# A long convolution with its tables loaded a stage earlier and its phases in another order, and seven projections whose first weights are loaded in the stage before

## What is computed

```python
def hyena_filters(L, fw1, fb1, fw2, fb2, fw3, freq):
    ...
    h = jnp.sin(fq * (z @ fw1.astype(F32) + fb1.astype(F32)))
    h = jnp.sin(fq * (h @ fw2.astype(F32) + fb2.astype(F32)))
    h = h @ fw3.astype(F32)
    ...
    return h * (decay + HY_SHIFT)

def hyena_mix(u, conv_w, conv_b, filt, bias):
    u = dwconv(u, conv_w) + conv_b
    x0, x1, v = jnp.split(u, 3, axis=-1)
    g = (v * x1).astype(F32)
    h = hyena_filters(L, *filt)
    hf, hb = h[:, :HY_WIDTH], h[:, HY_WIDTH:]
    k2 = jnp.concatenate([hf, jnp.zeros((1, HY_WIDTH), F32), hb[:0:-1]], axis=0)
    n = 2 * L
    y = jnp.fft.irfft(jnp.fft.rfft(g, n=n, axis=1) * jnp.fft.rfft(k2, axis=0)[None], n=n, axis=1)[:, :L]
    y = y + g * bias.astype(F32)
    return y.astype(u.dtype) * x0
...
def conv_ffn(h, w_up, conv_w, conv_b, w_down):
    g, u = jnp.split(h @ w_up, 2, axis=-1)
    g = dwconv(g, conv_w) + conv_b
    return (jax.nn.silu(g) * u) @ w_down
```

## Time and profile before

| what | value |
|---|---|
| median of three runs | 3491.16 us (3490.48 to 3492.16) |
| the profiled execution, its own time | 3485.01 us |
| its span | 3483.2 us |
| TensorE busy | 3002.3 us, 86% |
| VectorE, ScalarE, GpSimd busy | 49%, 35%, 5% |
| TensorE's mean granted clock | 0.927 of full speed |
| moved by DMA | 362.79 MB, mean 104 GB/s |

### The profile page before, as it was taken

One profiled execution on the slowest core, in us unless ns is written; L12 is line 12 of the kernel. 1 busy time (PEld: TensorE's weight loads), 2 busy tenths in 40 slices (PEclk: granted clock), 3 DMA queues, 4 the chain that ended last, 5 costly groups with the idle time before them and its releaser, 6 DMA issues. The chain is left out here.

```text
span 3483.2 us, 38114 instructions
## 1 busy us (share of the span) xinstructions
PE 3002.3 (86%) x14263; PEld 2349.5 (67%) x14263; DVE 1699.8 (49%) x2349; ACT 1214.2 (35%) x1614; POOL 164.8 (5%) x131
## 2 busy tenths in 40 slices
PE   6896788978999999978999999978857788499996
PEld 2382367767888887756777887857635566477775
DVE  1343332354576643424564443341366554488886
ACT  0220022233323232423333442233323322377774
POOL 0000000110001100000000000000000100221210
PEclk9997899899999999989999999989978898699998
DMA  6311011011235333101002221212200013399996
GB/s 244 113 48 64 19 49 49 1 37 73 92 122 169 113 123 100 67 19 45 7 2 96 97 96 68 89 43 85 72 7 1 1 49 146 140 350 350 343 339 241
DMA packets 76311, 362.79 MB, mean 104 GB/s; under 512 B 13428, under 2 KB 17347, under 8 KB 50596
## 3 DMA queue, kind: packets, MB, share of 16 engines
q1 hardware_dynamic: 62404, 327.69, 26.6%
q0 software_dynamic: 13792, 33.58, 2.8%
HBM read 360.68 MB, written 16.27 MB: 108 GB/s over the span
## 5 line engine op out<-in xcount | busy, mean ns | idle before, releaser
L288 PE MATMUL ps<-rounded,rounded 128*128 128x512 f32 (+3 forms) x3700 | 1374.0, 371 | 108.7 <-DVE rounded L1978 24.1
L289 PE MATMUL ps<-rounded,rounded 128*128 128x512 f32 (+3 forms) x3700 | 1334.6, 361 | 0.0
L290 PE MATMUL ps<-rounded,rounded 128*128 128x512 f32 (+3 forms) x3700 | 1332.9, 360 | 0.0
L288 PEld LDWEIGHTS ps<-rounded,rounded 128*128 128x128 f32 (+1 forms) x3700 | 703.8, 190 | 284.8 <-issue 69.5
L290 PEld LDWEIGHTS ps<-rounded,rounded 128*128 128x128 f32 (+1 forms) x3700 | 704.1, 190 | 107.3
L289 PEld LDWEIGHTS ps<-rounded,rounded 128*128 128x128 f32 (+1 forms) x3700 | 705.7, 191 | 95.0
L267 DVE TENSOR_TENSOR rounded<-work,rounded 128x1024 fp32r<-128x1024 f32 (+3 forms) x224 | 306.4, 1370 | 817.5 <-ACT rounded L263 817.0
L263 ACT CAST rounded<-work 128x1024 fp32r<-128x1024 f32 (+3 forms) x224 | 260.8, 1166 | 701.2 <-PE ps L290 561.9
L3125 DVE TENSOR_TENSOR rounded<-work,rounded 128x2048 fp32r<-128x2048 f32 x138 | 311.7, 2288 | 91.1 <-ACT rounded L2973 88.5
L2973 ACT CAST rounded<-work 128x2048 fp32r<-128x2048 f32 x138 | 258.6, 1909 | 83.6 <-PE ps L290 83.6
L274 PE MATMUL ps<-cst 128*128 128x256 f32 x544 | 157.8, 455 | 105.2 <-PEq L169 105.2
(11 more groups left out here) (435 smaller groups left out, 2587.3 us busy)
## 6 DMA issues: line engine op xcount, KB each, us to landing
work<-in_moe SPq DMA_DIRECT2D x138, 1024.0 KB, 7.3
work<-in_ffn_up SPq DMA_DIRECT2D x44, 1024.0 KB, 4.8
work<-in_ffn_down SPq DMA_DIRECT2D x66, 512.0 KB, 3.5
work<-in_ada_w SPq DMA_DIRECT2D x12, 2048.0 KB, 8.6
work<-in_ada_w POOLq DMA_DIRECT2D x48, 512.0 KB, 4.1
work<-in_w_out SPq DMA_DIRECT2D x16, 512.0 KB, 3.5
work<-in_w_gates SPq DMA_DIRECT2D x16, 512.0 KB, 3.6
work<-in_w_in_hy SPq DMA_DIRECT2D x12, 512.0 KB, 3.3
```

The lines of the kernel that those rows point to most:

```text
L288: k.nc.tensor.matmul(out, sh, mh, start=start, stop=False)
L289: k.nc.tensor.matmul(out, sh, ml, start=False, stop=False)
L290: return k.nc.tensor.matmul(out, sl, mh, start=False, stop=stop)
```

## The change

**The tables of the convolution** (`HyenaRooms`) are loaded by the projection before it, behind its first two weight tiles (`also` of `project_conv`): the latent tables, both decays, both positions and the three weight matrices. Only the four small tables of the context are still loaded inside `hyena`, when the latent filters are done.

**The order of the convolution** is written out as one list, `groups`. Both lengths go through the filter network's first two layers together (768 columns). The sequences are transposed and transformed between these layers; each spectrum is copied out of PSUM by ScalarE; then follow the filters, and the filters' spectra are multiplied by it as they come. The context's phases lie between the latent ones. Every group waits only for what it reads.

**Seven projections** get their first two weight tiles in the stage before: the output gate of the first block (`w_in_og`), `w_z_2`, `w_gates_2` and `w_xbc_2` of the last one, and the down projections (context and latent of layer 0, latent of layer 1). Their streams use semaphores of their own that are never cleared, so their counts start from `base`. The stage before issues the loads (`then.begin`) and splits both tiles in its last turn (`then.high`, `then.low`), ScalarE ahead of taking the product out of PSUM. The seven stages have no warm-up matmuls any more.

```diff
@@ class Stream
+    def begin(self, sp, before=None):
         for s in range(self.n):
+            if before:
+                sp.wait_ge(before.ready[s], before.base + before.tiles // before.n)
             sp.dma_start(self.raw[s], self.src[s]).then_inc(self.landed[s], 16)
+
+    def load(self, sp, begun=False):
+        if not self.ahead and not begun:
+            self.begin(sp)
@@ project_conv (project_act and ffn_down alike)
         def _(sp):
-            stream.load(sp)
+            if also:
+                stream.begin(sp)
+            for place, array in also:
+                sp.dma_start(place, array).then_inc(extra, 16)
+            stream.load(sp, bool(also))
+            if also:
+                sp.wait_ge(extra, 16 * len(also))
+            if then:
+                then.begin(sp, stream)
...
             if norm:
                 norm.sum_and_spread(pe)
-            else:
+            elif not stream.ahead:
                 keep_running(k)
...
-            for p in range(2):
+            for p in range(0 if stream.ahead else 2):
                 stream.high(act, p, 1)
...
                     if not last:
                         stream.high(act, p, i + 2)
+                    elif then:
+                        then.high(act, p, 1)
...
@@ ffn_up
+                    else:
+                        act.wait_ge(stream.ready[1], turns)
+                        then.high(act, p, 1)
@@ ffn_down
+            if then:
+                for p in range(2):
+                    then.low(dve, p, 1)
             dve.wait_ge(product[1], turns)
@@ hyena
+    groups = ([("layer1",)] + [("turn", 0, a) for a in range(4)] + [("turn", 1, a) for a in range(2)]
+              + [("forward", 0, 0), ("layer2",), ("forward", 0, 1)] + [("filter", 0, a) for a in range(4)]
+              + [("forward", 0, 2), ("forward", 0, 3)] + [("spectrum", 0, f) for f in range(4)]
+              + [("filter", 1, a) for a in range(2)] + [("forward", 1, f) for f in range(2)]
+              + [("back", 0, c) for c in range(2)] + [("spectrum", 1, f) for f in range(2)]
+              + [("back", 0, c) for c in range(2, HYT)] + [("back", 1, c) for c in range(HYT)])
+    of_act = [group[0] in ("turn", "forward") for group in groups]
...
         def _(sp):
+            sp.wait_ge(filtered, 4)
+            for j in range(4):
+                sp.dma_start(rooms.tab_ctx[j], k.dram["hy_dft_ctx"][j]).then_inc(tables, 16)
...
+            for n, group in enumerate(groups):
+                if n >= 4:
+                    need(cleared[n - 4])
+                products(group).then_inc(done, 1)
...
+                if group[0] == "layer1":
+                    act.wait_ge(argued, 1)
+                    nc.scalar.activation(rooms.sine1, rooms.arg, ACT.Sin).then_inc(sined, 1)
```

More of the change, by code:

```diff
@@ L799, in _, with ffn_up @@
             in_turns(dve, turns, turn)
-def ffn_up(k, layer, hidden, scratch, segs, norm, beside=None):
+def ffn_up(k, layer, hidden, scratch, segs, norm, then, beside=None):
     nc = k.nc
@@ L916, in _, with ffn_down @@
                 mixer_gains(k, 1, next_mod, ((0, 1), (0,)))
-def ffn_down(k, weights, hidden, mod, seg):
+def ffn_down(k, weights, hidden, mod, seg, then=None):
     nc = k.nc
@@ L1044, in hyena @@
+def hyena(k, u, rooms):
     nc = k.nc
     k.stage()
[L1046 to L1059 removed]
@@ L1063, in hyena, with bank @@
+    at = {group: n for n, group in enumerate(groups)}
+    of_act = [group[0] in ("turn", "forward") for group in groups]
+    cleared = [(by_act if mine else by_dve, of_act[:n + 1].count(mine)) for n, mine in enumerate(of_act)]
+    def bank(group, part=0, n=BANK):
+        return k.bank(2 * (at[group] % 4) + part, n)
     with k.block() as block:
@@ L3171, in build, with ffn @@
         k = Kernel(nc, ctx, dram)
+        def ffn(layer, mod, norm, segs, **more):
+            at, half = MEM - 6 * 2 * D, 2 * D
+            places = [at, at + D], [(at + half, at + half + D), (at + 2 * half, at + 2 * half + D)]
+            down = [Stream(k, f"ffn_down_{layer}", D, ahead=True, places=places) for seg in segs]
+            ffn_up(k, layer, hidden, scratch, segs, norm, down[0], **more)
+            for n, seg in enumerate(segs):
+                ffn_down(k, down[n], hidden, mod, seg, down[n + 1] if n + 1 < len(segs) else None)
         def gain(a):
```

397 lines of the change are left out of this document (198 added, 199 removed).

## The result

| | before | after |
|---|---|---|
| median, side by side on one chip | 3491.66 us (3490.48 to 3499.89) | 3405.21 us (3397.14 to 3407.58) |
| the profiled execution, its own time | 3485.01 us | 3397.14 us |
| its span | 3483.2 us | 3395.4 us |
| TensorE's mean granted clock | 0.927 | 0.934 |

Four runs each; the ratio is 0.9742, 95% interval 0.9723 to 0.9762, and the medians are 86.5 us apart. The forecast was 3402, its range 3385 to 3424.

What follows compares the result with a forecast made beforehand. TensorE, busy 86%, was taken as the bound, with time to win where it idles or runs at half clock. Convolution 64.4 plus joints 24.5 gave 89 us off 3485.0, 3396; with 6.2 for the timed median, 3402; range 3385 to 3424.

Steps and rivals of the forecast that it cites:

- Convolution: Long convolution: tables already there and groups reordered, so the next stage starts at 404.2 instead of 468.56, 64.4 us earlier.
- The front: Convolution's start: VectorE's product, sine argument, sine and ScalarE's four copies come before the first transform, which can start at 281.5.
- TensorE to be the bound: Convolution from the first transform on: TensorE's 133.5 full matmuls set the pace, 115 us, while VectorE keeps up.
- The 4 us for the 64-row filters: Convolution's filters, using 64 of 128 rows, may let the clock fall amid full matmuls: 4 us charged, bounds 0 and 9.
- the restart: Start of the convolution's first transform: TensorE begins at half clock after idle time, charged 2.5 us.
- The rival with the tables in the way: Projection before the convolution: third weight tile lands 10 us later than reckoned, projection stands 8 us; 3410 us, chance 2%.
- The seven joints: Between projections: first weight tiles fetched and split a stage ahead save 32.5 us; 24.5 after clock terms, bounds 15 and 36.
- The charge of 10 us for real matmuls that take the restart: Behind the four long joints: without warm-ups, real matmuls run at low clock, 1.5 to 3.3 us each, 10 us lost.
- The term of 2 us for the short joints: Behind the three short joints: idle time shrinks from 3 or 4 us to 2.8, so the clock restart costs 2 us less.
- The kinder clock: Rival: the convolution's filters keep 2.4 GHz (-4 us) and restarts cost only 1.5 (-5 us); 3393 us, chance 18%.
- The joints give little: Rival: every restart takes 3.3 us, tails grow 2.3, joints save some 8, convolution loses another 3; 3421 us, chance 17%.
- stay at 1.2 GHz without warm-ups: Rival, slower than before: TensorE keeps half clock through the projections, 181 us more on three stretches; 3583 us, chance 2%.

Runs made afterwards that it cites:

- again_2: The changed kernel run once more without a change: 3406.20 us, ratio 0.9733 to the kernel before.
- ahead_only: The kernel before with only the seven joints changed, its convolution loading its own tables; run twice: 3476.16 and 3472.11 us, ratios 0.9946 and 0.9935.
- before_warm_filters: The kernel before with 11 warm-up matmuls (7 for the short size) put just ahead of the convolution's filters: 3492.40 us, ratio 0.9986.

## Why the prediction was right

**Convolution: forecast 64.4 us earlier, measured 70.3, of which 1.6 were there before the stage began; the stage itself gave 68.6, 4.2 more than forecast.** The front was right to half a microsecond: the first transform could start 12.1 us into the stage and did at 11.7, held by the sine and ScalarE's copies as described. *TensorE to be the bound* held, with no wait at all behind it. Three terms were mis-sized, two of them of the clock, and together they make 4.0 of these 4.2 us. The 4 us for the 64-row filters did not occur: they ran 7.13 us for 16 records, as full matmuls do, and the window around them was granted 1.00:

```profile
296.40:303.60 7.20, 7.20 (x18) 2.97 (x17) 4.63 (x7) 1.07 (x2) 0.00 (x0) 1.00 0.01 2
```

And the restart cost 1.5 us (8.60 for the 7.13 of the later 16 records), not 2.5, the smaller of the two rows I had. I chose the row that was nearest by instruction; nearest by the idle time before it (4.5 us there, 3.9 here) would have been right. The third went the other way: without the restart TensorE worked for 116.0 us, where I had reckoned 115. The Trainium skill ("TensorE: Matmul & The Clock Gate", Part 1) says that a busy TensorE releases the throttle; by that the 4 us were not to be expected. Here its outcome was the right one. But the earlier trace rows still stand against it as a rule, and so do the 24 us of `again_2` at half clock with TensorE fully busy.

**The projection before it: forecast 0.** It has no idle time between its first product and its last in the changed kernel, with the third tile issued behind all the tables. The rival with the tables in the way fell.

**The seven joints: gaps forecast at 5.8, 8.4, 7.3, 6.9 and three times 2.8 us, measured 5.89, 8.28, 7.26, 6.96 and three times 2.81.** The 32.5 us between the products went as reckoned. By position the joints gave 26.2 us (96.5 less 70.3) up to the first product of `w_xbc_2`, where 24.5 were forecast; in `ahead_only`, freed of the slow attention, 24 to 25. The charge of 10 us for real matmuls that take the restart held: over the first 10 us behind the four long joints the clock is 0.72, 0.77, 0.76 and 0.79, where it was 1.00 behind each of them before, 9.6 us lost (an estimate: the missing share of the clock times 10 us). The term of 2 us for the short joints was a little small: 0.83, 1.00 and 0.83 for 0.71, 0.83 and 0.83, by the same estimate 2.9. The first of them, at `w_z_2`, against the earlier trace rows:

```profile
2278.67:2288.67 10.00, 10.00 (x37) 8.09 (x38) 1.22 (x1) 3.88 (x4) 0.00 (x0) 0.83 0.30 106
```

**The sum** was 89 us off the profiled execution, measured 87.9. That it fits so well is partly luck: the convolution gave 4.2 us more than forecast and the joints 2 more, 1.6 were there before the convolution, and against them 7.0 were lost in the state-space stage and the router and 1.7 in smaller steps, which no step of mine had. At the medians the fit is 3402 to 3405.

**The rivals.** The kinder clock was right in its mechanism inside the convolution, and the longer state-space stage and router took back its gain. *The joints give little* was wrong for the joints; the 3472 and 3476 us of `ahead_only` would have spoken for it if only medians had been read. TensorE did not stay at 1.2 GHz without warm-ups.

**Open.** What makes an execution take the slow or the fast way through the latent attention was not found. The kernel with the changed joints alone was slow there and in the last attention both times (125.16 and 123.09 us for 115.93). By my own test that would belong to this variant. But `before_warm_filters`, which has none of the new joints, was slow in both as well, 156.43 and 123.04 us. So the new joints are not needed for it; whether the position of earlier work weighs the odds, these profiles can't tell.

## What to carry to other kernels

When a stage waits for a load, first rewrite the order of its groups so that each waits only for what it reads: here that gave 50 us, with the copies moved to ScalarE, and the early fetch 18. If weights are fetched a stage ahead, move the warm-up matmuls to the end of the stage before, where they lie under the tail of VectorE; leaving them out cost 6 to 10 us by position over seven joints, and leaving them at the head of a stage whose weights are there cost more (9 us over the first three joints). Compare two profiles stage by stage and check the granted clock of stages that nobody touched, before a difference of 10 us in the spans is given a reason.

## What the hardware showed that I had not expected

- One kernel, one stage, two lengths: 147.26 and 156.97 us for the latent attention, at 1.00 and 0.92 mean clock; in `again_2` the loss lies in the first 30 us of the stage, where some of the matmuls use 64 rows and the others 128. The filters, also of 64 rows, ran at 1.2 GHz for 14.0 us when they came after idle time, and at 2.4 GHz (7.1 us) when they came behind 22 warm-up records or in the midst of transforms. So in these traces the filters alone did not lift a low clock and kept a high one. Whether the 64 rows have a part in the attention's slow way is not shown.
- The state-space stage took 47.9, 52.0 or 55.9 us, the router 32.6 or 35.7, in the same kernels: steps, not a spread. Together with the attention stages they move a whole execution by 10 to 20 us.
